# Latent attention: sums of squares of three key pairs as two products of rounded parts, behind the head's second scores

## What is computed

```python
def rms_norm_2(x, g):
    xf = x.astype(jnp.float32)
    y = xf * lax.rsqrt(jnp.mean(xf * xf, axis=-1, keepdims=True) + EPS)
    return (y * g.astype(jnp.float32)).astype(x.dtype)
...
        kv = (rms_norm_2(c_kv, g_ckv[l]) @ w_ukv[l]).reshape(B, L, MLA_HEADS, QK_NOPE + V_DIM)
        k_nope, v_a = kv[..., :QK_NOPE], kv[..., QK_NOPE:]
        k_r = jnp.broadcast_to(k_rope[:, :, None, :], (B, L, MLA_HEADS, QK_ROPE))
        k = jnp.concatenate([k_nope, k_r], axis=-1)
        q = rms_norm_2(q, g_qn[l])
        k = rms_norm_2(k, g_kn[l])
        q = jnp.concatenate([q[..., :QK_NOPE], rotary(q[..., QK_NOPE:], cos, sin)], axis=-1)
        k = jnp.concatenate([k[..., :QK_NOPE], rotary(k[..., QK_NOPE:], cos, sin)], axis=-1)
        attn = dense_bidirectional_attention(q, k, v_a)
```

## Time and profile before

| | us |
|---|---|
| median of 3 runs | 1674.89 |
| lowest, highest | 1674.73, 1675.24 |
| profiled execution | 1675.06 |
| its span in the trace | 1673.3 |
| TensorE busy | 1667.3 (100%) |
| VectorE busy | 1029.0 (61%) |
| ScalarE busy | 638.6 (38%) |
| GpSimd busy | 713.3 (43%) |
| stretch of the latent attention's heads | about 1277 to 1371 |

### The profile page before, as it was taken

One profiled execution on the slowest core, in us unless ns is written; L12 is line 12 of the kernel. 1 busy time (PEld: TensorE's weight loads), 2 busy tenths in 40 slices (PEclk: granted clock), 3 DMA queues, 4 the chain that ended last, 5 costly groups with the idle time before them and its releaser, 6 DMA issues.

```text
span 1673.3 us, 21109 instructions
## 1 busy us (share of the span) xinstructions
PE 1667.3 (100%) x7640; PEld 1363.7 (81%) x7640; DVE 1029.0 (61%) x1237; ACT 638.6 (38%) x895; POOL 713.3 (43%) x303
## 2 busy tenths in 40 slices
PE   9999999999999999999999999999999999999999
PEld 7887888887788887888888888888778768888887
DVE  7767566526565458367665567776574753969451
ACT  5222222226665756321322322213446744333321
POOL 2444344434333431444444344434356533444443
PEclk9999999999999999999999999999999999999999
DMA  5332232325511320342433323332252033323343
GB/s 199 101 110 90 81 101 93 107 90 197 139 64 53 99 76 26 101 138 90 141 97 103 103 88 100 103 103 89 93 193 76 26 124 104 95 94 101 94 142 117
DMA packets 44192, 173.14 MB, mean 103 GB/s; under 512 B 5033, under 2 KB 5417, under 8 KB 42828
## 3 DMA queue, kind: packets, MB, share of 16 engines
q1 hardware_dynamic: 39024, 148.13, 27.2%
q10 hardware_dynamic: 5084, 23.82, 4.2%
HBM read 159.22 MB, written 10.62 MB: 101 GB/s over the span
## 4 chain that ended last, share of the span: by engine, by line
PE 96%; DVE 2%; ACT 1%; issue 0%; DMA 0%; POOL 0%; SPq 0%; DVEq 0%; ACTq 0%; POOLq 0%
PE psum L339 26%; PE psum L340 26%; PE psum L344 26%; PE psum L1297 1%; PE psum L331 1%; PE psum L333 1%; PE psum L332 1%; PE psum L363 1%; PE psum L366 1%; PE psum L399 1%; PE psum L1883 1%; PE psum L400 1%; PE psum L404 1%; PE psum L369 1%; PE psum L1860 1%; PE psum L1287 1%
## 5 line engine op out<-in xcount | busy, mean ns | idle before, releaser
L274 POOL TENSOR_TENSOR wlo<-raw,whi 128x1024 fp32r<-128x1024 f32 (+2 forms) x256 | 657.9, 2570 | 866.5 <-ACT whi L319 865.9
L319 ACT ACTIVATE whi<-raw 128x1024 fp32r<-128x1024 f32 (+2 forms) x259 | 286.1, 1105 | 699.8 <-PE psum L344 633.8
L339 PE MATMUL psum<-h_hi,whi 128*128 128x512 f32 x1304 | 515.1, 395 | 0.1
L340 PE MATMUL psum<-h_lo,whi 128*128 128x512 f32 x1304 | 507.9, 389 | 0.0
L344 PE MATMUL psum<-h_hi,wlo 128*128 128x512 f32 x1304 | 324.4, 389 | 0.0
L339 PEld LDWEIGHTS psum<-h_hi,whi 128*128 128x128 f32 x1304 | 244.9, 188 | 55.2 <-issue 4.9
L340 PEld LDWEIGHTS psum<-h_lo,whi 128*128 128x128 f32 x1304 | 244.9, 188 | 52.3 <-issue 2.6
L344 PEld LDWEIGHTS psum<-h_hi,wlo 128*128 128x128 f32 x1304 | 244.8, 188 | 50.9
L725 DVE TENSOR_TENSOR silu<-sig,gate 128x512 f32<-128x512 f32 x44 | 100.3, 2279 | 41.8 <-ACT sig L670 41.8
L339 PE MATMUL psum<-mid_hi,whi 128*128 128x512 f32 x308 | 120.1, 390 | 0.0
L340 PE MATMUL psum<-mid_lo,whi 128*128 128x512 f32 x308 | 119.8, 389 | 0.0
(11 more groups left out here) (423 smaller groups left out, 2504.6 us busy)
## 6 DMA issues: line engine op xcount, KB each, us to landing
raw<-wk_dram SPq DMA_DIRECT2D x220, 512.0 KB, 3.5
raw<-wd_dram SPq DMA_DIRECT2D x32, 704.0 KB, 4.1
raw<-wp_dram SPq DMA_DIRECT2D x8, 640.0 KB, 3.8
x_scratch<-xT ACTq DMA_DIRECT2D x2, 2048.0 KB, 8.5
spectra_scratch<-spec_out ACTq DMA_DIRECT2D x4, 1024.0 KB, 6.4
xT<-x_scratch ACTq DMA_DIRECT2D x8, 512.0 KB, 4.5
spec<-spectra_scratch ACTq DMA_DIRECT2D x2, 2048.0 KB, 10.3
xT<-x_dram SPq DMA_DIRECT2D x4, 512.0 KB, 7.5
```

The lines of the kernel that those rows point to most:

```text
L274: pool.tensor_tensor(wlo[s][:, 0:w], raw[s][:, 0:w], whi[s][:, 0:w].bitcast(F32), ALU.subtract).then_inc(lo_ready, 1)
L319: act.activation(whi[s][:, 0:w], raw[s][:, 0:w], ACT.Copy).then_inc(hi_ready, 1)
L339: pe.matmul(dst, a, m_hi[:, c, :], start=start and c == chunks[0][0], stop=False)
L340: pe.matmul(dst, a, m_lo[:, c, :], start=False, stop=False)
```

## The change

Pair 0 stays as it was. For pairs 1 to 3, ScalarE squares bank 1 twice, first into a new rounded tile `sq_k_hi`, then into `sq_k` as before. VectorE subtracts one from the other into `sq_k_lo` (`vector_key_low`), behind its query product at the end of an even head. TensorE sums both parts with a rounded `block_ones_r`, which takes the place of an unused mask in the constants, in two products of rounded numbers, and does so behind the head's second scores instead of ahead of them. The new tiles lie where `stage32` is (in the trace, scratch; used only ahead of the heads). The transfers of the rope tables count on `const_landed` instead of a semaphore of their own.

```diff
@@ -123,7 +123,7 @@
         small = keep("small", [P, 96])
         psum = ctx.enter_context(nc.psum_tensor("psum", [P, 8 * 512], F32))
         ident, block_ones, ones, before = (constf[:, i, :] for i in range(4))
-        ident_r, neg_tri, neg_ones, mask_qk, mask_kq = (constr[:, i, :] for i in range(5))
+        ident_r, neg_tri, neg_ones, mask_qk, block_ones_r = (constr[:, i, :] for i in range(5))
         head_sq = [square, sumsq]
         idle_zeros = raw[0][:, D:FH * P]
 
@@ -205,6 +205,8 @@
         rope_sum = nc.alloc_sbuf_tensor_at("rope_sum", [P, T], F32R, offset=scratch0 + 2 * 1024)
         lat_sq = [square, sumsq, *(at(86 + 2 * i, f"lat_sq{i}", [P, T]) for i in range(3))]
         lat_factor = [rstd, at(102, "lat_factor", [P, T])]
+        sq_k_hi, sq_k_lo = (nc.alloc_sbuf_tensor_at(f"sq_k_part{i}", [P, T], F32R, offset=scratch0 + (8 + 2 * i) * 1024)
+                            for i in range(2))
         kr32 = mprob[1][:, 0, :]
         tab_k, k_turn, k_shift = (at(a, f"k_part{a}", [P, T]) for a in (98, 100, 104))
 
@@ -411,7 +413,6 @@
         x_stored = sem("x_stored")
         vec_landed = sem("vec_landed")
         const_landed = sem("const_landed")
-        rope_landed = sem("rope_landed")
         constr_ready = sem("constr_ready")
 
 
@@ -1723,6 +1724,7 @@
                  self.key_sq, self.sum, self.key_sum, self.q_factor, self.k_factor) = (
                     sem(f"mla_{x}") for x in ("projected", "q32", "k32", "k_rotated", "q_hi", "q_lo", "k_hi", "k_lo",
                                               "squares", "key_squares", "sums", "key_sums", "q_factor", "k_factor"))
+                self.key_low = sem("mla_key_square_low")
                 (self.scores, self.neg, self.exped, self.normed, self.turned, self.copied0,
                  self.copied1, self.out, self.y, self.y_hi, self.ready) = (
                     sem(f"mla_{x}") for x in ("scores", "negated", "exped", "normed", "transposed",
@@ -1741,9 +1743,9 @@
                 return small[:, a:a + 4]
 
             def load(self, act):
-                act.dma_start(rope[:, :], rope_in).then_inc(rope_landed, 16)
+                act.dma_start(rope[:, :], rope_in).then_inc(const_landed, 16)
                 for a, b, n in ((0, 96, 32), (32, 64, 32), (64, 0, 64)):
-                    act.dma_start(rope_odd[a:a + n, :], rope_in[b:b + n, :]).then_inc(rope_landed, 16)
+                    act.dma_start(rope_odd[a:a + n, :], rope_in[b:b + n, :]).then_inc(const_landed, 16)
 
             def tensor_latents(self, pe):
                 u = BASE["mla_cq"]
@@ -1814,13 +1816,18 @@
                 last.then_inc(unit_done if first else self.total, 1)
 
             def tensor_key_sum(self, pe, p):
-                pe.wait_ge(self.key_sq, p + 1)
+                pe.wait_ge(self.key_sq, 2 * p + 1)
                 if p:
                     pe.wait_ge(self.q_factor, 4 * p - 1)
                 else:
                     pe.wait_ge(self.z, 3)
                     pe.wait_ge(self.turn, 15)
-                pe.matmul(bank(2), block_ones, sq_k[:, :], start=True, stop=False)
+                if p:
+                    pe.wait_ge(self.key_low, p)
+                    pe.matmul(bank(2), block_ones_r, sq_k_hi[:, :], start=True, stop=False)
+                    pe.matmul(bank(2), block_ones_r, sq_k_lo[:, :], start=False, stop=False)
+                else:
+                    pe.matmul(bank(2), block_ones, sq_k[:, :], start=True, stop=False)
                 pe.matmul(bank(2), neg_ones, rope_sum[:, :], start=False, stop=True).then_inc(self.key_sum, 1)
 
             def tensor_query_sum(self, pe, h):
@@ -1902,10 +1909,10 @@
                         self.tensor_scores(pe, h, 0)
                     if h:
                         self.tensor_turn(pe, h - 1, 1)
-                        if h % 2 and h + 1 < HEADS:
-                            self.tensor_key_sum(pe, (h + 1) // 2)
                     if scores_ahead < 2:
                         self.tensor_scores(pe, h, 1)
+                    if h % 2 and h + 1 < HEADS:
+                        self.tensor_key_sum(pe, (h + 1) // 2)
                     if h:
                         self.tensor_turn(pe, h - 1, 2)
                     else:
@@ -2003,6 +2010,7 @@
                 act.wait_ge(self.projected, 2 * p + 1)
                 if p:
                     act.wait_ge(self.key_sum, p)
+                    act.activation(sq_k_hi[:, :], bank(1), ACT.Square).then_inc(self.key_sq, 1)
                 act.activation(sq_k[:, :], bank(1), ACT.Square).then_inc(self.key_sq, 1)
 
             def scalar_query_square(self, act, h):
@@ -2127,7 +2135,7 @@
 
             def vector_latents(self, dve):
                 low, high = slice(HD, QKD), slice(QKD, P)
-                dve.wait_ge(rope_landed, 64)
+                dve.wait_ge(const_landed, 176)
                 dve.tensor_scalar(tab_q[:, :], rope[:, :], col("g_qn"), QKD ** -0.5, ALU.mult,
                                   ALU.mult).then_inc(self.turn, 1)
                 dve.tensor_scalar(tab_k[HD:P, :], rope[HD:P, :], vec[HD:P, VEC["g_kn"]:VEC["g_kn"] + 1], None,
@@ -2188,6 +2196,11 @@
                 dve.scalar_tensor_tensor(k32s[h % 2][rows, :], bank(1)[rows, :], vec[rows, gain:gain + 1], rstd[rows, :],
                                          ALU.mult, ALU.mult).then_inc(self.k32, 1)
 
+            def vector_key_low(self, dve, p):
+                dve.wait_ge(self.key_sq, 2 * p + 1)
+                dve.tensor_tensor(sq_k_lo[:, :], sq_k[:, :], sq_k_hi[:, :].bitcast(F32),
+                                  ALU.subtract).then_inc(self.key_low, 1)
+
             def vector_v(self, dve):
                 dve.wait_ge(self.total, 4)
                 for t in range(2):
@@ -2250,6 +2263,8 @@
                     self.vector_norm(dve, h)
                     if h + 2 < HEADS:
                         self.vector_query(dve, h + 2)
+                        if h % 2 == 0:
+                            self.vector_key_low(dve, h // 2 + 1)
                 self.vector_y(dve, HEADS // 2 - 2)
                 self.vector_copy(dve, HEADS - 1, 1)
                 self.vector_copy(dve, HEADS - 1, 3)
@@ -3181,8 +3196,7 @@
     constf = np.stack([eye, blocks, np.ones((P, P), np.float32), before], 1)
     tri = -(i[:, None] >= i[None, :]).astype(np.float32)
     mask_qk = np.where(i[None, :] > i[:, None], np.float32(NEG), np.float32(0))
-    mask_kq = np.where(i[:, None] >= i[None, :], np.float32(NEG), np.float32(0))
-    constr = np.stack([eye, tri, -np.ones((P, P), np.float32), mask_qk, mask_kq], 1)
+    constr = np.stack([eye, tri, -np.ones((P, P), np.float32), mask_qk, blocks], 1)
     pos = np.arange(T, dtype=np.float32)
     inv = (np.float32(ROPE_THETA) ** (-np.arange(0, ROPE, 2, dtype=np.float32) / np.float32(ROPE))).astype(np.float32)
     ang = (pos[:, None] * inv[None, :]).astype(np.float32)
```

## The result

The changed kernel takes 1676.89 us (median of 22 runs, 1676.53 to 1679.19); the kernel before, on the same chip, 1675.07 us (22 runs, 1674.68 to 1676.58). The ratio is 1.0014, with a 95% interval of 1.0008 to 1.002: slower by 1.8 us, inside what I had called no change, and close to the 1676.8 forecast. In 7 of the 22 executions, the profiled one among them, TensorE's clock was not granted in full all the time (mean 0.998 or 0.999), and these took 1678.15 to 1679.19; the other 15 have a median of 1676.81, which is +1.74.

What follows compares the result with a forecast made beforehand. TensorE was taken to bound the kernel, except in head 1, where ScalarE and VectorE decide. Pair 1's +2.37 less 2 x 0.24 gave +1.89 us, a median of 1676.8, range 1675.2 to 1678.1.

Steps and rivals of the forecast that it cites:

- Heads 3 and 5, TensorE: Key sums of pairs 2 and 3: of 0.40 us saved on TensorE, 0.24 is kept in each head.
- Pair 1, ScalarE: End of head 0: one more square pushes everything behind it on ScalarE by 0.48 us.
- Pair 1, VectorE: New subtraction, held by GpSimd's L274, ends 0.55 us after it, at 1291.34, instead of taking 0.69.
- Who waits: Head 1: first maximum and all behind it 2.37 us later; TensorE stands about 1.7 us before the key sum.
- Pairs 2 and 3: VectorE at the ends of heads 2 and 4: subtraction fits the gaps, ending 0.14 us before head 5's maximum.
- The sum: Whole kernel: +2.37 at pair 1 less 2 x 0.24 at the later pairs, +1.89 us.
- the clock rival: TensorE's clock falls in head 1's stall, to 1.2 GHz until 1299 us: up to 8 us, 1684.8; chance 3%.
- Hidden after all: Head 1's delay is taken up somewhere and TensorE keeps 3 x 0.40: -1.2 us, 1673.7; chance 5%.
- No lock: Pair 1's subtraction takes 0.69 us despite GpSimd: +0.77 us in all, 1675.7; chance 16%.
- Two GpSimd operations ahead of VectorE: Pair 1's subtraction waits for L274 and the query's low part: +3.65 less 0 to 0.48, 1678.1 to 1678.5; 6%.

Runs made afterwards that it cites:

- experiment 1: Changed kernel with pair 1 put back as before, only pairs 2 and 3 by parts; 1674.62 us against 1675.01 for the kernel before (ratio 0.9997).
- experiment 7: Kernel with only pairs 2 and 3 by parts, plus first scores of heads 4 and 6 put ahead of the transposes; 1674.34 us (ratio 0.9996).
- experiment 8: Kernel before the change, with only the first scores of heads 4 and 6 put ahead of the transposes; 1674.82 us (ratio 0.9999).
- experiment 2: Pair 1 alone by parts, pairs 2 and 3 as in the kernel before; 1677.52 us (ratio 1.0018).
- experiment 4: Changed kernel with a needless 0.68 us copy on VectorE just ahead of pair 1's subtraction; 1676.91 us (ratio 1.0014).
- Experiment 6: Changed kernel with the key sums of all three pairs back ahead of the second scores; 1677.92 us (ratio 1.0016).
- experiment 9: Changed kernel with seven extra rounded products on TensorE filling the wait before pair 1's key sum; 1676.73 us (ratio 1.001).
- experiment 10: Changed kernel with key sums back ahead of the second scores and ten extra rounded products filling TensorE's wait; 1676.79 us (ratio 1.001).
- experiment 3: Changed kernel with the unrounded square written to PSUM, so the subtraction has one operand in SBUF instead of two; 1675.69 us (ratio 1.0005).
- experiment 5: Changed kernel with the subtraction of all three pairs on GpSimd instead of VectorE; 1675.44 us (ratio 1.0003).

## Why the prediction was right, and where it was not

**Heads 3 and 5, TensorE.** At the fourth scores of head 3 0.36 was in hand, where I had 0.24: I had taken the second exponential as unmoved, since it stands behind the key factor. It began 0.11 earlier, because the second scores now run ahead of the key sum. This changed nothing at the end, since the row scaling leaves 0.24, the number that I had taken for another reason as well. Experiments 1, 7 and 8 show the scaling to be that limit, in part.

**Pair 1, ScalarE**: a step of 0.48 and everything behind it 0.48 later, as said. **Pair 1, VectorE**: 0.55 behind GpSimd's end, as said, in six kernels (the changed one and experiments 2, 4, 6, 9 and 10; in 9, GpSimd's operation ran from 1288.27 for 2.40). The cost of 2.28 stands beside 2.37: I took the subtraction's end plus 0.02 as the maximum's start, while the maximum's recorded start lies 0.07 before that end. Experiment 3 shows that the cause is the second SBUF operand; experiment 4 that GpSimd's end decides. **Who waits**: the wait of TensorE was 1.65 us, forecast 1.7.

**Pairs 2 and 3** on VectorE: 0.68 in head 3; 1.77 in head 5, ending just ahead of the maximum, as said. The key factor was not late.

**The sum.** At the full clock +1.74 measured, +1.89 forecast. The difference is the 0.09 at pair 1 and scatter. The whole set of executions has +1.82.

**The step that failed is the clock rival.** I gave it 3% and up to 8 us. It occurred in 7 of 22 executions, and it cost 1.3 to 2.4 us in each (1678.15 to 1679.19 against 1676.81). The chance was wrong because I argued that TensorE "never stood as long as 1.7 us in this stage"; that says what was not tried in the trace, not what would not happen. And I took it for a thing that happens or not for a kernel, while it happens in some of its executions. The price was wrong because I let the lower clock last from the standstill to 1299 us, 8 us of it, and counted each of them in full. In the profiled execution it was below 1.00 in three rows of 2 us only, in a part of two of them, and it came after the stretch that I had named. Experiment 6 has it in that stretch, in two rows of 2 us, and pays 0.9 us. The median of all 22 escaped it, since less than half of them were slowed; that 1676.89 lies so near to 1676.8 owes something to this. With the key sum in its old place the median would not have: 1677.92.

The Trainium skill, "TensorE: Matmul & The Clock Gate", Part 1, has the lower level as the state to which TensorE returns when it is idle. Experiments 9 and 10 agree in so far as the fall went when the idle time was filled; that the fall shows some 10 us after the wait (within 3 us in experiment 6) is explained by none of these runs. The same part says that the point at which the clock rises differs between runs of one kernel; whether the 7 of 22 at the fall are of the same kind is not shown.

**The rivals.** Hidden after all: no, +2.43 for pair 1 alone. No lock: not in the changed kernel, but made in experiment 3, +0.62 for +0.77. Two GpSimd operations ahead of VectorE: did not occur. GpSimd's next operation, L2296, began at 1290.82 and lasted 1.72 instead of 1.28; this time it was the one that was held, while VectorE finished.

## What to carry over

A saving on the engine that is always busy is worth nothing where that engine waits for the others; cost each place of a repeated edit by the chain at that place, and apply it only where it pays (pairs 2 and 3 here, -0.4 us; pair 1, +2.3). Before a VectorE operation with two SBUF operands goes next to a GpSimd operation, take its price as "until GpSimd's end", or put one operand into PSUM (1.87 us to 0.68 here). And price a new standstill of TensorE twice, once by its length and once by the executions in which the clock falls after it; work whose result nobody needs took most of the second price away in the two kernels where it was tried.

## What the runs showed of the hardware that I had not expected

- After a standstill of TensorE of 1.65 us, in a stretch where it also idles now and then, its clock fell in a third of the executions, and after one of 2.33 us in most. In the profiled execution of the changed kernel the wait ended at 1291.55 and the first lower clock stands in the row from 1302. With the wait filled it was none of 11 and one of 11. It costs 1.3 to 2.4 us each time in the changed kernel.
- The lock goes both ways. VectorE's subtraction waited for GpSimd's L276, and then GpSimd's L2296 was held for 0.44 by it (1.72 instead of 1.28). With the subtraction's operand in PSUM that operation took 1.28 again (experiment 3).
- By the records the subtraction ends 0.55 after GpSimd's operation, where it takes 0.68 undisturbed, so the two overlap by 0.13. No run explains this; it held in six kernels.
- VectorE's row scalings, with one operand in SBUF and the result there, are held as well: four of them took 2.86 us instead of 1.79 with one more GpSimd operation beside them, and 2.75 instead of 1.67 in head 2 (experiment 5).
- The subtraction takes about twice as long on GpSimd (1.27 to 1.61 against 0.68) and was still better placed there than on VectorE beside a busy GpSimd: +0.35 us against +1.74.
